# Three quarters of two output tiles moved in between the last attention steps

## Chip, cores and metric

The kernel runs on one core of one Trainium2 chip. The metric is the device time of one execution in microseconds (us); lower is better. TensorE (PE in the profile) multiplies matrices into PSUM, ScalarE (ACT) and VectorE (DVE) work between PSUM and SBUF, GpSimd (POOL) works on SBUF, and SyncE (SP) issues the weight loads.

## The reference, cut to what matters

Three blocks run one after the other on a sequence of 512 tokens with 1024 features. The second block has two layers, each of them a feed-forward part, an attention part and another feed-forward part; the third block has one attention part. The change concerns the three places where attention ends and its output projection begins:

```
# second block, each layer: four differential heads (d) and four pairs of forget-gate heads (f)
x = x + concat([o_f, o_d]) @ w_out        # o_f: features 0 to 511, o_d: features 512 to 1023
x = x + 0.5 * swiglu(rmsnorm(x))          # the next feed-forward part
# third block: gated recurrence (lru) and four pairs of block attention heads (m)
x = x + gate * (concat([y_lru, y_att]) @ w_out)   # y_att: features 512 to 1023
```

## The kernel before, in words

Activations lie transposed: feature tiles of 128 partitions by 512 tokens. Each float32 product is made of three matmuls on rounded parts: high weight by high input, high weight by low input, low weight by high input (`products`, lines 1467 to 1469). So an output tile of 128 features over four input tiles is 12 matmuls of 128x512, and over eight it is 24.

One program is written once as a sequence of calls on an object `on`; it is run five times, once for each engine, and every engine issues its own instructions in that order. No engine overtakes within its queue. Semaphore events tie them together: `wait_ge` names the event that an instruction waits for.

A weight tile goes through three steps: a DMA brings it to one of five raw buffers, ScalarE rounds it into a high part (line 1904), GpSimd subtracts for the low part (line 3181). Both are issued two units ahead of the projection that needs them (`LOOK` is 2), and around these projections there are three slots for rounded weights, so the tile that is three further on takes the slot of the one just used. A call of `T` issues the rounding of the unit two behind it, then the matmuls.

`attend` writes the order of one attention by hand. A job is one pair of heads and one block of 128 query tokens. Its steps are `scores` (line 1817), softmax on VectorE and ScalarE, `weigh`, `turn` (transposes on TensorE, line 1827, then two ScalarE copies out of PSUM, line 2267) and `gather` (weights times values, line 1844). The two buffers that the copies write are shared by all jobs, so the copies of one job wait for the gather of the job before. In the loop a job is turned in the pass before the one that gathers it. `beside` is a generator of other projections that fill TensorE between the steps; near the end it issues the eight tiles `outd` (or `outl`) of the other half of the output projection. The last pair of heads takes its blocks in the order 3, 2, 1, 0.

When a pair of heads is done, `head_out` makes its high part on ScalarE (line 2000) and its low part on VectorE (line 2427). In the third block VectorE first applies a gate (line 3058), and `head_parts` does the rounding. A matmul on input tile c waits for the low part of c.

After `attend` the eight output tiles follow. In the second block `renew` follows each tile: VectorE adds it to the residual (line 2890), ScalarE scales and rounds it, VectorE makes the sums and low parts that the next feed-forward part takes. The call for tile n rounds the weights of tile n+2 on ScalarE, between the `renew` of tile n-1 and that of tile n. In the third block VectorE adds (line 3156) and SyncE stores.

Of the kernel before, what the change touches and what calls it, by code (L numbers as in the profile page):

```python
# [11 lines left out]
S = 512  # L12
# [166 lines left out]
class Dry:  # L179
# [5 lines left out]
    def wait_ge(self, sem, n):  # L185
        return self
# [11 lines left out]
NRAW, LOOK, LEAD = (5, 2, 2)  # L198
# [712 lines left out]
        return ('o', self.tag, *h)  # L911


def attend(on, at, beside):

    scored = weighed = turned = gathered = 0
    total = len(at.jobs)
    pair = lambda j: at.jobs[j][0][0] != 'd'
    while gathered < total:
        if scored < total and pair(scored):  # L920
            if weighed < scored:
                on.weigh(at, *at.jobs[weighed])
                weighed += 1
            on.scores(at, *at.jobs[scored])
            scored += 1
        elif scored < total:
            on.scores(at, *at.jobs[scored])
            scored += 1
        if turned > gathered and (pair(gathered) or turned - gathered > 1 or scored == weighed == turned):
            h, qt = at.jobs[gathered]  # L930
            on.gather(at, h, qt)
            gathered += 1
            if qt == at.blocks(h)[-1]:
                on.head_out(at, h)
                at.out += 1
        if weighed < scored and (scored == total or scored - weighed > 1):
            on.weigh(at, *at.jobs[weighed])
            weighed += 1
        two = turned < total and pair(turned)
        if two:  # L940
            next(beside, None)
        if weighed > turned and (two or weighed - turned > 2 or scored == weighed):
            on.turn(at, *at.jobs[turned])
            turned += 1
        next(beside, None)
    for _ in beside:
        pass


def second(on, k, layer, m):  # L950
    L, scale = (str(layer), m.scale)
# [36 lines left out]
    at = Heads(k, L, [('d', i) for i in range(4)] + [('f', i) for i in range(4)], k.P2, [last, ('lambda', L), ('forgot', L)])  # L988
# [5 lines left out]
    def projections():  # L994

        ready = None

        def enter():
            if ready is not None and ready[0] == 'dqk':
                on.diff_in(L, ready[1], R, last)  # L1000
                on.rope_moves(L, ready[1])
            elif ready is not None:
                on.fox_in(L, ready[1], R, last)
        for name, n in [('dqk', n) for n in (2, 6, 3, 7)] + [('fqk', n) for n in (0, 4, 1, 5, 2, 6, 3, 7)]:
            on.T_part((name, L, n), name + L, n, A, 0, 2)
            enter()
            yield
            on.T_part((name, L, n), name + L, n, A, 1, 2)
            if ready is not None and ready[0] == 'dqk':
                on.rope(L, ready[1])  # L1010
            ready = (name, n)
            yield
        enter()
        yield
        for i in range(4):
            on.diff_parts(at, i)
            if i % 2:
                yield
        for n in range(KT):
            on.T(('outd_' + L, n), 'out' + L, n, at.OA, kt=4, first=4)  # L1020
            on.part(res, n, ('outd_' + L, n))
            yield
            yield
# [10 lines left out]
    def both():  # L1034
        one, two = (projections(), norms())
        while next(one, 'end') != 'end':
            next(two, None)
            yield
    attend(on, at, both())
    m = Ffn('f2_' + L, 'f2i' + L, 'f2o' + L, res.A, res.sum, None, [('filled', ('out2_' + L, 7))], clear=('filled', ('out2_' + L, 0)), before=res)  # L1040
    res.later = (0, 1, 2, 3)
    for n in range(KT):
        on.T(('out2_' + L, n), 'out' + L, n, at.OA, kt=4)
        renew(on, res, n, ('out2_' + L, n), ('filled', ('fqk', L, 7)), m, 0)
    scale = res.sum
    nxt = banked(Sum('fin2' if layer else 'f1_1', k.R[1 - layer], S, ('fox', L, 7), range(8) if layer else (), 2 if layer else 0, [('lo', ('mid', 'f2_' + L), FF - 1)]))
# [19 lines left out]
def third(on, k, res):  # L1066
    last = ('filled', ('d', 'f2_1', 7))
    on.norm3_gain()
    A = k.XA('n3')
    m = Norm(res.twin, k.X, lambda j: ('x', 'f2_1', j), A, lambda j: k.sm[:, j:j + 1], lambda j: k.ada3[:, j:j + 1], [last, ('gain3',)], keep=True, bank=True)  # L1070
    on.roots(res.twin, 4)
    for j in range(1, 11):
        norm(on, m, j)
        if j == 3:
            on.roots(res.sum, 2)
    on.row(res.sum)
    on.lru_loads(last)
    on.lru_rate()
    for n in range(4):
        if n == 0:  # L1080
            on.T2((('xl', 0), 'z3', 0), (('xl', 1), 'z3', 1), A)
        if n > 1:
            on.T(('xl', n), 'z3', n, A)
        on.lru_in(n, last)
        on.lru('taps', n)
        on.final_tile(res, n, 'final2')
    beside = {0: [('gate', 0, 0), ('gate', 0, 1), ('gate', 1, 0), ('gate', 1, 1)], 4: [('gate', 2, 0), ('gate', 2, 1), ('gate', 3, 0), ('gate', 3, 1)], 1: [('decay', 0), ('decay', 1)], 5: [('decay', 2), ('decay', 3)], 6: [('root', 0), ('root', 1), ('root', 2), ('root', 3)]}
    heads = iter([[], [], [(0, 0), (4, 0)], [], [(0, 1), (4, 1)], [(4, 2), (1, 0), (5, 0)], [(1, 1), (5, 1)], [(5, 2), (2, 0), (6, 0)], [(2, 1), (6, 1)], [(6, 2), (3, 0), (7, 0)], [(3, 1), (7, 1)], [(7, 2)]])
    for i, n in enumerate((0, 4, 1, 5, 2, 6, 3, 7)):
        on.T(('z', n), 'z3', 8 + n, A)  # L1090
        on.head_in(n, last)
        for step in beside.get(n, []):
            on.lru(*step)
        if i < 4:
            on.final_tile(res, 4 + i, 'final2')
        for step in next(heads):
            on.head(*step)
    for kp in range(4):
        on.K('v3', 'v3', 0, A, kp, 4)
        for step in next(heads):  # L1100
            on.head(*step)
    for tt in range(4):
        on.value3(tt, last)
    at = Heads(k, 'm', [('m', i) for i in range(4)], k.P3, [last, ('headed', 7), ('head scale', 3), ('lru mult', 3), ('rate',)])
    at.OA, at.old = (k.XA('y3'), [('filled', ('gl', 3))])
    out = Residual('out3', lambda j: k.ada3[:, 16 + j:17 + j], None)

    def projections():

        ready = None  # L1110
        for i in range(8):
            name, w, n = ('gl', 'z3', i - 4) if i > 3 else ('ga', 'ga3', i)
            on.T_part((name, n), w, i, A, 0, 2)
            if ready is not None:
                on.gate_in3(*ready)
            if i > 4:
                on.lru_gate(i - 5)
            yield
            on.T_part((name, n), w, i, A, 1, 2)
            if i % 2:  # L1120
                on.lru('scan', i // 2)
            ready = (name, n)
            yield
        on.gate_in3(*ready)
        on.lru_gate(3)
        for n in range(4):
            on.lru_out(at, n)
            if n % 2:
                yield
        on.head_parts(at, 0)  # L1130
        on.head_parts(at, 1)
        yield
        for n in range(KT):
            on.T(('outl', n), 'out3', n, at.OA, kt=4)
            on.part(out, n, ('outl', n))
            yield
        on.head_parts(at, 2)
    attend(on, at, projections())
    on.head_parts(at, 3)
    for n in range(KT):  # L1140
        on.T(('out3', n), 'out3', n, at.OA, kt=4, first=4)
        on.store(n)


class Engine:


    def __init__(self, k, e, done):
        self.k, self.e, self.done, self.seen = (k, e, done, {})
        self.pos = self.h = 0  # L1150

    def wait_ge(self, *event):

# [41 lines left out]
    def pair(self, m, i):  # L1195

        upper = self.unit('upper', ('T', m.wi, i, 0), 1024)
        lower = self.unit('lower', ('T', m.wi, FF + i, 0), 1024)
        return (m.tag, i)
# [9 lines left out]
    def T_part(self, key, name, n, X, part, of):  # L1209
        if part == 0:  # L1210
            self.weights(*self.unit('split', ('T', name, n, 0), 1024))

    def K(self, key, name, n, X, kp, ntok):
        self.weights(*self.unit('split', ('K', name, n, kp), 1024))
# [204 lines left out]
class Tensor(Engine):  # L1419
# [27 lines left out]
    def T_part(self, key, name, n, X, part, of):  # L1447

        k, w = (self.k, 8 // of)
        if part == 0:  # L1450
            self.open = self.unit('split', ('T', name, n, 0), 1024)
        i, h = self.open
        out = self.bank(*key) if part else self.take(k.banks, *key, hold=True)
        m = self.products(out, i, h, X, range(w * part, w * part + w), 0, S, 0, 7)
        if part == of - 1:
            m.then_inc(*k.filled.inc(('used', h), ('filled', key)))
            k.banks.let(key)

# [1917 lines left out]
```

## Time and profile before

| what | value |
|---|---|
| median of three runs | 3398.5 us |
| the runs | 3394.53, 3398.5, 3404.37 us |
| the profiled execution's own time | 3406.11 us |
| its span | 3404.3 us |
| TensorE matmul, busy share of the span | 97% |
| VectorE, GpSimd, ScalarE | 55%, 48%, 43% |

In a timeline row the first number is the start from the beginning of the span and the second the duration; in brackets is the time for which the engine sat idle just before and the instruction that released it. Matmuls overlap in the pipeline, so the distance between starts, not the duration, is what one costs.

### The profile page before, as it was taken

The numbers are of one execution on the slowest core, as the hardware profiler recorded it, in microseconds if no ns is written. First come the engines' busy times: TensorE is split into PE (matmuls) and PEld (weight loads), VectorE is DVE, ScalarE is ACT, GpSimd is POOL, SyncE is SP. The second block draws the span as 40 slices with busy tenths as digits, with TensorE's granted clock in tenths as the row PEclk, the third lists the DMA queues.
The fourth block names the chain that finished last, engine by engine and source line by source line (L and its number), as shares of the span: only waits on it lengthen the run. The fifth ranks groups of instructions, "written<-read, shape, count | busy, mean of one in ns | idle before, by whom it ended". The sixth has DMA issues, their size and how long they took to land.

```text
span 3404.3 us, 47159 instructions
## 1 busy us (share of the span) xinstructions
PE 3312.1 (97%) x18750; PEld 2801.7 (82%) x18750; DVE 1880.4 (55%) x3348; ACT 1468.2 (43%) x2582; POOL 1644.4 (48%) x952
## 2 busy tenths in 40 slices
PE   8999999999999999999998999999999999999998
PEld 5767788887888889988777999899987769998776
DVE  4366775523222376842667576557624667582555
ACT  4533323523322363533556354444434555352543
POOL 4313445564544455655415565455546246564332
PEclk9999999999999999999999999999999999999999
DMA  7212333442344423334202323332343123333211
GB/s 284 69 49 62 97 96 126 151 148 71 128 153 144 142 87 100 112 100 121 75 32 86 104 100 104 94 113 88 106 112 109 32 60 111 100 103 105 72 62 56
DMA packets 102218, 345.96 MB, mean 102 GB/s; under 512 B 12173, under 2 KB 12557, under 8 KB 101838
## 3 DMA queue, kind: packets, MB, share of 16 engines
q1 hardware_dynamic: 101200, 341.10, 31.1%
q8 instruction: 148, 2.42, 0.3%
q10 hardware_dynamic: 798, 1.85, 0.2%
q14 instruction: 72, 0.59, 0.1%
HBM read 336.08 MB, written 2.10 MB: 99 GB/s over the span
## 4 chain that ended last, share of the span: by engine, by line
PE 87%; DVE 6%; ACT 4%; issue 1%; POOL 1%; DMA 1%; SPq 0%; DVEq 0%; ACTq 0%; POOLq 0%
PE ps L1467 16%; PE ps L1468 16%; PE ps L1469 16%; PE ps L1503 8%; PE ps L1505 8%; PE ps L1504 8%; PE ps L1530 2%; PE ps L1532 2%; PE ps L1531 2%; PE ps L1817 2%; PE ps L1844 1%; POOL t L3181 1%; PE ps L1827 1%; ACT t L1919 1%; DMA t<-in_w_ada 1%
## 5 line engine op out<-in xcount | busy, mean ns | idle before, releaser
L3181 POOL TENSOR_TENSOR t<-t,t 128x1024 fp32r<-128x1024 f32 (+2 forms) x408 | 931.9, 2291 | 1261.4 <-ACT t L1904 1248.8
L1467 PE MATMUL ps<-t,t 128*128 128x512 f32 x2608 | 1045.0, 401 | 13.4 <-POOL t L3181 8.1
L1468 PE MATMUL ps<-t,t 128*128 128x512 f32 x2608 | 1023.3, 392 | 0.0
L1469 PE MATMUL ps<-t,t 128*128 128x512 f32 x2608 | 1021.7, 392 | 0.0
L3191 POOL TENSOR_TENSOR t<-t,t 128x512 fp32r<-128x512 f32 x440 | 570.4, 1325 | 388.4 <-ACT t L1919 388.4
L1503 PE MATMUL ps<-t,t 128*128 128x256 f32 x2464 | 699.0, 284 | 22.2 <-DVE ps L2477 9.4
L1504 PE MATMUL ps<-t,t 128*128 128x256 f32 x2464 | 693.8, 282 | 0.0
L1505 PE MATMUL ps<-t,t 128*128 128x256 f32 x2464 | 693.5, 281 | 0.0
L1467 PEld LDWEIGHTS ps<-t,t 128*128 128x128 f32 x2608 | 492.8, 189 | 141.0 <-issue 24.2
L1469 PEld LDWEIGHTS ps<-t,t 128*128 128x128 f32 x2608 | 492.6, 189 | 108.3
L1468 PEld LDWEIGHTS ps<-t,t 128*128 128x128 f32 x2608 | 493.2, 189 | 99.4 <-issue 1.7
L1904 ACT CAST t<-t 128x1024 fp32r<-128x1024 f32 (+2 forms) x412 | 398.7, 976 | 348.8 <-PE ps L1469 211.2
L1503 PEld LDWEIGHTS ps<-t,t 128*128 128x128 f32 x2464 | 464.6, 189 | 28.3 <-issue 10.7
L1505 PEld LDWEIGHTS ps<-t,t 128*128 128x128 f32 x2464 | 467.7, 190 | 0.0
L1504 PEld LDWEIGHTS ps<-t,t 128*128 128x128 f32 x2464 | 466.3, 189 | 0.2
L1919 ACT CAST t<-t 128x512 fp32r<-128x512 f32 x440 | 255.4, 620 | 207.1 <-DVE t L2450 186.8
L1919 ACT CAST t<-ps 128x512 fp32r<-128x512 f32 x176 | 103.5, 588 | 140.9 <-DVE ps L2440 106.5
L2260 ACT ACTIVATE t<-ps,t 128x128 f32<-128x128 f32 (+3 forms) x160 | 86.6, 544 | 177.9 <-DVE t L3024 66.5
L2721 DVE SCALAR_TENSOR_TENSOR ps<-t,t,ps 128x392 f32<-128x392 f32 (+14 forms) x232 | 159.1, 686 | 6.2
L2450 DVE TENSOR_TENSOR t<-t,ps 128x512 f32<-128x512 f32 x176 | 119.8, 681 | 48.5 <-PE ps L1505 46.4
L1530 PE MATMUL ps<-t,t 128*128 128x512 f32 x336 | 134.7, 401 | 8.0 <-DVE t L2629 4.3
L2457 DVE TENSOR_TENSOR t<-ps,t 128x512 fp32r<-128x512 f32 x176 | 120.7, 686 | 28.8 <-ACT t L1919 25.3
(331 smaller groups left out, 3637.6 us busy)
## 6 DMA issues: line engine op xcount, KB each, us to landing
t<-in_w_f1i SPq DMA_DIRECT2D x88, 512.0 KB, 3.7
t<-in_w_f2i SPq DMA_DIRECT2D x88, 512.0 KB, 3.8
t<-in_w_ada SPq DMA_DIRECT2D x72, 512.0 KB, 4.3
t<-in_w_ffi SPq DMA_DIRECT2D x44, 512.0 KB, 3.7
t<-in_w_f1o SPq DMA_DIRECT2D x32, 512.0 KB, 4.0
t<-in_w_f2o SPq DMA_DIRECT2D x32, 512.0 KB, 4.0
t<-in_w_gate SPq DMA_DIRECT2D x24, 512.0 KB, 4.0
t<-in_w_out SPq DMA_DIRECT2D x48, 256.0 KB, 2.6
```

Of the source, the lines that this page charges most:

```text
L1467: e.matmul(out, wh[:, at], X.hi[c][:, 0:N], start=c == first, stop=False)
L1468: e.matmul(out, wh[:, at], X.lo[c][:, 0:N], start=False, stop=False)
L1469: m = e.matmul(out, wl[:, at], X.hi[c][:, 0:N], start=False, stop=c == final)
L1503: e.matmul(out, wh[:, at], m.A.hi(j, x), start=opens and j == 0, stop=False, skip_group_check=not opens)
L1504: e.matmul(out, wh[:, at], m.A.lo(j, x), start=False, stop=False, skip_group_check=not opens)
L1505: mm = e.matmul(out, wl[:, at], m.A.hi(j, x), start=False, stop=j == 3, skip_group_check=not opens)
L1530: e.matmul(out, X.hi[c][:, at], wh[:, w], start=c == 0, stop=False)
L1904: e.copy(k.WH[k.slot[n]][:, 0:w], k.raw[:, j % NRAW, 0:w]).then_inc(*k.rounded.inc(('rounded', j)))
L1919: e.copy(four(piece_at(k, k.WH, m, i, piece)), src).then_inc(*k.rounded.inc(('rounded', m.tag, i, piece)))
L2721: e.scalar_tensor_tensor((c3 if j == 30 else a3)[:, :, lo:hi], h3[:, :, lo + w - 15:hi + w - 15], param(k, 'conv_w', w * 8 + i), a3[:, :, ...
L3181: e.tensor_tensor(k.WL[k.slot[n]][:, 0:w], k.raw[:, j % NRAW, 0:w], f(k.WH[k.slot[n]][:, 0:w]), ALU.subtract).then_inc(*k.rest.inc(('rest' ...
L3191: e.tensor_tensor(four(piece_at(k, k.WL, m, i, piece)), src, four(f(piece_at(k, k.WH, m, i, piece))), ALU.subtract).then_inc(*k.rest.inc(( ...
```

## The change

Of output tiles 0 and 1 the products over the first three of the four input tiles (the first three pairs of heads) are issued inside the last passes of the loop in `attend`, through a second generator `fill`. One step of it is one input tile for one output tile: three matmuls. There are six steps in each attention. One step is taken after each gather once all scores are issued, and two after each turn. After `attend`, tiles 0 and 1 only get their products over the last pair of heads. Their two PSUM banks are held from the first step on. All three attentions are changed; the number of instructions is not.

```diff
-def attend(on, at, beside):
+def attend(on, at, beside, fill):
...
             if qt == at.blocks(h)[-1]:
                 on.head_out(at, h)
                 at.out += 1
+            if scored == total and gathered < total:
+                next(fill, None)
...
             on.turn(at, *at.jobs[turned])
             turned += 1
+            if scored == total:
+                next(fill, None)
+                next(fill, None)
         next(beside, None)
     for _ in beside:
         pass
+    for _ in fill:
+        pass
+
+
+def begun(on, at, name, w, first):
+
+    for c in range(first, first + 3):
+        for n in range(2):
+            on.T_some((name, n), w, n, at.OA, (c,), first=first)
+            yield
...
-    attend(on, at, both())
+    attend(on, at, both(), begun(on, at, 'out2_' + L, 'out' + L, 0))
...
     for n in range(KT):
-        on.T(('out2_' + L, n), 'out' + L, n, at.OA, kt=4)
+        if n < 2:
+            on.T_some(('out2_' + L, n), 'out' + L, n, at.OA, (3,))
+        else:
+            on.T(('out2_' + L, n), 'out' + L, n, at.OA, kt=4)
         renew(on, res, n, ('out2_' + L, n), ('filled', ('fqk', L, 7)), m, 0)
...
-    attend(on, at, projections())
+    attend(on, at, projections(), begun(on, at, 'out3', 'out3', 4))
     on.head_parts(at, 3)
     for n in range(KT):
-        on.T(('out3', n), 'out3', n, at.OA, kt=4, first=4)
+        if n < 2:
+            on.T_some(('out3', n), 'out3', n, at.OA, (7,), first=4)
+        else:
+            on.T(('out3', n), 'out3', n, at.OA, kt=4, first=4)
         on.store(n)
...
@@ class Engine
+    def T_some(self, key, name, n, X, ks, first=0, kt=4):
+
+        if ks[0] == first:
+            self.opened[key] = self.unit('split', ('T', name, n, first), 128 * kt)
+            i, h = self.opened[key]
+            self.weights(i, h - LOOK)
+        if ks[-1] == first + kt - 1:
+            self.weights(*self.opened[key])
...
@@ class Tensor(Engine)
+    def T_some(self, key, name, n, X, ks, first=0, kt=4):
+
+        k, final = (self.k, first + kt - 1)
+        if ks[0] == first:
+            self.opened[key] = self.unit('split', ('T', name, n, first), 128 * kt)
+        i, h = self.opened[key]
+        out = self.take(k.banks, *key, hold=True) if ks[0] == first else self.bank(*key)
+        m = self.products(out, i, h, X, ks, first, S, first, final)
+        if ks[-1] == final:
+            m.then_inc(*k.filled.inc(('used', h), ('filled', key)))
+            k.banks.let(key)
```

## Rows read from the trace of the kernel before

**Rows 1.** The page: busy time, share of the span, instructions.

```profile
PE 3312.1 (97%) x18750; PEld 2801.7 (82%) x18750; DVE 1880.4 (55%) x3348; ACT 1468.2 (43%) x2582; POOL 1644.4 (48%) x952
```

**Rows 2.** Busy time by stretch: end of attention, layers 0 and 1; then eight output tiles.

```profile
1791.92:1801.09 9.17, 6.95 (x79) 5.22 (x77) 2.66 (x12) 5.29 (x15) 1.28 (x1) 1.00 0.08 29
2761.24:2770.41 9.17, 6.95 (x79) 5.22 (x77) 2.65 (x12) 5.29 (x15) 1.28 (x1) 1.00 0.12 29
1801.09:1823.78 22.69, 22.69 (x99) 17.66 (x97) 15.57 (x33) 16.56 (x33) 15.89 (x12) 1.00 0.39 127
```

**Rows 3.** Timeline of TensorE, layer 0: the last turns and gathers, output tiles 0 and 3.

```profile
1791.92 1.09 PE L1827 MATMUL ps<-t,t 128*128 128x128 f32 x8
1793.26 1.09 PE L1844 MATMUL ps<-t,t 128*64 128x128 f32 x16 [0.24 <-ACT t L2267]
1794.29 0.88 PE L1827 MATMUL ps<-t,t 128*128 128x128 f32 x6
1795.61 1.09 PE L1844 MATMUL ps<-t,t 128*64 128x128 f32 x16 [0.45 <-ACT t L2267]
...
1800.72 0.44 PE L1844 MATMUL ps<-t,t 128*64 128x128 f32 x4 [0.61 <-ACT t L2267]
1801.09 0.50 PE L1467 MATMUL ps<-t,t 128*128 128x512 f32 x1
...
1809.45 0.40 PE L1467 MATMUL ps<-t,t 128*128 128x512 f32 x1
```

**Rows 4.** Timeline of ScalarE in the same stretch.

```profile
1794.39 1.07 ACT L2267 COPY t<-ps 128x512 f32<-128x512 f32 x2 [0.57 <-PE ps L1844]
1795.35 0.60 ACT L2000 CAST t<-ps 128x512 fp32r<-128x512 f32 x1
...
1801.19 0.59 ACT L2000 CAST t<-ps 128x512 fp32r<-128x512 f32 x1 [0.62 <-PE ps L1844]
...
1807.23 0.62 ACT L1904 CAST t<-t 128x512 fp32r<-128x512 f32 x1
```

**Rows 5.** Timeline of VectorE in the same stretch.

```profile
1795.99 0.69 DVE L2427 TENSOR_TENSOR t<-ps,t 128x512 fp32r<-128x512 f32 x1 [1.58 <-ACT t L2000]
1801.82 0.69 DVE L2427 TENSOR_TENSOR t<-ps,t 128x512 fp32r<-128x512 f32 x1 [5.14 <-ACT t L2000]
1804.15 0.69 DVE L2890 SCALAR_TENSOR_TENSOR t<-ps,t 128x512 f32<-128x512 f32 x1 [1.65 <-PE ps L1469]
```

**Rows 6.** Timeline of GpSimd in the same stretch: low parts of weights.

```profile
1791.95 1.28 POOL L3181 TENSOR_TENSOR t<-t,t 128x512 fp32r<-128x512 f32 x1 [2.97 <-ACT t L1904]
...
1807.93 1.30 POOL L3181 TENSOR_TENSOR t<-t,t 128x512 fp32r<-128x512 f32 x1 [4.26 <-ACT t L1904]
```

**Rows 7.** Timeline of TensorE, third block: the last gathers, output tiles 0 and 1.

```profile
3372.31 0.88 PE L1844 MATMUL ps<-t,t 128*64 128x128 f32 x12 [1.70 <-ACT t L2267]
...
3374.62 1.12 PE L1844 MATMUL ps<-t,t 128*64 128x128 f32 x8 [0.84 <-ACT t L2267]
...
3376.82 0.70 PE L1844 MATMUL ps<-t,t 128*64 128x128 f32 x4 [0.46 <-ACT t L2267]
3377.44 0.79 PE L1467 MATMUL ps<-t,t 128*128 128x512 f32 x1
...
3381.87 0.40 PE L1467 MATMUL ps<-t,t 128*128 128x512 f32 x1
```

**Rows 8.** Timeline of VectorE, third block: low part of the last heads.

```profile
3378.92 0.69 DVE L2427 TENSOR_TENSOR t<-t,t 128x512 fp32r<-128x512 f32 x1 [0.68 <-ACT t L2000]
```

**Rows 9.** Busy time by stretch; the column after POOL's is the granted clock.

```profile
1832.00:1834.00 2.00, 0.81 (x6) 0.60 (x6) 2.00 (x4) 2.00 (x5) 2.00 (x2) 1.00 0.00 0
1834.00:1836.00 2.00, 1.04 (x5) 1.04 (x6) 2.00 (x2) 0.69 (x2) 2.00 (x2) 0.65 0.00 0
3374.00:3376.00 2.00, 1.38 (x10) 1.04 (x10) 0.52 (x3) 0.48 (x2) 0.00 (x0) 0.51 0.00 0
3380.00:3382.00 2.00, 2.00 (x8) 1.59 (x8) 0.00 (x0) 0.00 (x0) 0.76 (x1) 0.79 0.00 0
```

More of the change, by code:

```diff
@@ L1150, in __init__ @@
         self.pos = self.h = 0
+        self.opened = {}
     def wait_ge(self, *event):
```

## Prediction

> **What bounds the kernel now.** First the page: TensorE is busy for 97% of the span and no other engine for more than 55% [rows 1]. So time can only be won where TensorE idles or runs at the lower of its two clock levels, and it is lost wherever a new wait stands in its queue. Then the busy time of the stretches that the change touches: from the transposes behind the last scores to the first output tile TensorE is busy 6.95 of 9.17 us, in both layers alike, so 2.2 us are idle; in the eight output tiles behind it TensorE idles for nothing [rows 2]. Then TensorE's timeline of the end of attention [rows 3]: turns and gathers alternate, and each gather waits 0.24 to 0.61 us for ScalarE's copies. ScalarE's own copies wait for the gather before [rows 4], since two buffers are shared: gather, copies, gather is one chain, and the transposes stand beside it. In the third block the waits before gathers are longer, 1.70, 0.84 and 0.46 us [rows 7].
>
> About 0.3%, 10.2 us, is what a measurement of this kernel can tell from no change.
>
> **The change, part by part.** No instruction is added or removed. The weight loads, their rounding and the low parts on GpSimd stay at their places in each queue: the weights of output tiles 0 and 1 are ready before the fills (GpSimd ends the second at 1793.23 [rows 6]; with one fill and eight transposes ahead of it that weight is wanted at about 1793.7), so SP, ScalarE and GpSimd get nothing new to wait for there. The two PSUM banks come from finished jobs. I cost these edits at nothing; if the weight came late, its first user would wait under 1 us.
>
> *One fill.* From 1801.09 to 1809.45 lie 36 matmuls of the kind [rows 3]: 0.232 us each, three cost 0.70, the six fills of an attention 4.18.
>
> *First gap in a layer.* Three fills, 2.09 us, stand before the gather that began at 1793.26; 0.24 of idle takes part of it. The gather starts 1.85 later.
>
> *Second gap.* Before the next gather come one fill, a turn and two fills on the third input tile. That tile is what the gather at 1793.26 finishes. Its low part was there at 1795.99 + 0.69 = 1796.68 [rows 5], behind the two copies and the rounding on ScalarE [rows 4]: 3.42 after the gather's start. TensorE gets there after gather (1.03), fill (0.70) and turn (0.88), 2.61. It stalls 0.81, then does two fills, and the gather comes 3.42 + 1.39 = 4.81 after the one before instead of 2.35: 2.46 later. Queued behind that stall are the gather, and through the shared buffers the next copies, so everything behind moves too. The fills are used up here; the three later gaps stay as they are. Attention ends 1.85 + 2.46 = 4.31 later, for 4.18 of work moved.
>
> *The cover that goes.* Before, the last heads' output was rounded while TensorE did three quarters of tile 0: the low part came at 1801.82 + 0.69 = 1802.51 [rows 5], 1.42 after TensorE began the tile, and nothing was seen of it. Now the only products left in tiles 0 and 1 need just this part: TensorE stalls 1.42. After 1.39 more for both tiles, tile 2 takes 2.78.
>
> *The weights of tile 3.* Their rounding stands on ScalarE behind the renewal of tile 0 (at 1807.23, [rows 4]); GpSimd ends at 1809.23 [rows 6] and TensorE begins tile 3 at 1809.45 [rows 3]: 0.22 to spare. The renewal starts with VectorE's addition, 3.06 after the start of the output tiles now [rows 5], 0.51 after the start of the tile's twelfth matmul; in the new order it is 1.42 + 0.46 + 0.51 = 2.39, so 0.67 sooner, but from a start 4.31 later: 3.64 late. The weights come at 1812.87, TensorE is free at 1805.40 + 1.42 + 1.39 + 2.78 = 1810.99. It stalls 1.9, and tile 3 begins 3.4 late. From there weights and tiles run in step as before.
>
> The sum for one layer: new stalls 0.81 + 1.42 + 1.9 = 4.1, less the idle that is filled, 0.24 + 0.45 = 0.7: 3.4 on TensorE; by the renewal's start 3.6. I take 3.5. The bounds: 0, if ScalarE, idle for 22.69 - 16.56 = 6.1 us of the output tiles [rows 2], lets the renewals catch up; and 3.6 with no catching up. I take a value near the upper, because each rounding stands behind a renewal and comes with 0.22 to spare. Behind the tiles, in the first products of the feed-forward part, VectorE is busy throughout while TensorE is 0.81 of 2.00 us [rows 9]: a delay handed to VectorE is not made good there.
>
> *Third block.* The idle filled is 0.84 + 0.46 = 1.30. The first three input tiles are long finished, so there is no stall between the fills. The cover is worse: the last heads' low part is ready at 3378.92 + 0.69 = 3379.61 [rows 8], 2.17 after output tile 0 began [rows 7]. No renewal follows, and the rounding for tile 2 (about 1.9 us behind the last high part, by the lengths in [rows 4, 6]) comes just as tiles 0 and 1 end. So 0.9 is lost at an unchanged clock. The clock is half in this stretch: the granted clock is 0.51 in 3374 to 3376 and 0.79 in 3380 to 3382 [rows 9], which puts the half level, 1.2 GHz, from about 3374.0 to 3380.8. Tile 0 took 4.43 there instead of 2.78 [rows 7], 1.65 lost. With TensorE filled from 3372.31 on the full level may return sooner: all of it would make -0.8, none +0.9. I take 0, the middle.
>
> A rule weighed: the TensorE clock. [Rows 9] show TensorE busy 0.81 of 2.00 us, and in the next two the granted clock at 0.65; [rows 2] show 2.2 us of idle, in pieces up to 0.61, over 9.17 us at 1.00. The new stalls, 0.61 and 1.42 with one short gather between and then 1.9, lie between the two. The Trainium skill (TensorE: Matmul & The Clock Gate, A second HAM failure mode) tells of a kernel whose short idles between groups of matmuls let the clock swing between the two levels. By that rule each layer would come out as in rival A; the trace agrees with it in [rows 9] and not in [rows 2].
>
> The sum: 2 x 3.5 + 0 = +7.0. The profiled execution would go from 3406.1 to 3413.1. It lies 7.6 above the median of the runs shown; the difference is carried over, 3398.5 + 7.0 = 3405.5.
>
> **The rivals.**
>
> A: the clock falls at the new stalls; slower. The place is output tiles 0 to 5 of each layer. A half-clock stretch as long as that in the third block, 6.8 us, costs up to 3.4; one that takes only a tile's worth, 1.65. For it speaks the 1.70 of idle before the clock at 0.51 [rows 7, 9], against it [rows 2]. It decides from one tile's worth in each layer on: 7.0 + 3.3 = 10.3. At the full price it is 7.0 + 6.8 = 13.8: 3412.
>
> B: the delay is made good. ScalarE's 6.1 us of idle lets the renewals catch up, TensorE's stall at tile 3 shrinks, and the change does almost nothing: +1, 3399.5. Against it: the 0.22 to spare.
>
> C: the fills do what they seem to do. All idle before gathers is filled and no stall takes its place: at most 2.2 + 2.2 + 1.3 = 5.7, with the clock of tile 0 7.4, short of 10.2. A middle of -3 gives 3395.5. It needs the last low part not to be waited for, and the rows say that it is.
>
> **How the numbers follow.** The forecast (+4 to +10, no clock stretch that counts) 0.45, A 0.37, B 0.12, C 0.06. The time is the forecast's, 3405.5. The range goes from 3397, which leaves out most of C, to 3416, A with a third stretch. Slower by over 0.3% is A, 0.37; faster is the edge of C, 0.02; within 0.3% is the rest, 0.61.
>
> **What would show it.** Right: in the new trace no idle before the gather that began at 1793.26; a wait of TensorE for line 2427 of about 0.8 between fills, and of about 1.4 (2.2 in the third block) before the last quarter of tile 0; a wait for line 3181 of near 1.9 at tile 3; attention's end 4.3 later. Wrong: tile 3 without a wait (then B), the granted clock under 1.00 in output tiles 0 to 5 (then A), or no wait for line 2427 (then C). A half-clock stretch elsewhere that comes or goes between executions would shift the time by a like amount without the change having caused it.

## The result and the profile after

The changed kernel took 3406.7 us (median of 11 runs, 3404.99 to 3413.29), the kernel before 3398.5 (11 runs, 3394.29 to 3404.37). The ratio is 1.0024 [1.0016, 1.0032]: 8.2 us slower, 5.4 to 10.9 by the interval. The forecast was 3405.5, 7.0 slower than before and so within 0.3% of it. The prediction took 10.2 us as the least that a measurement of this kernel can tell from no change; with eleven runs of each kernel 8.2 can be told as well.

The profiled execution took 3405.18 us with a span of 3403.4, 0.9 under that of before, although the median rose. As the prediction says, the profiled execution of before lay 7.6 above its median; that of after lies 1.5 below. So whole spans say nothing here, and what follows compares **stages**: from the start of the last scores of an attention to the first product of the next feed-forward part, and in the third block to the end of VectorE's last addition. The last scores of layer 0 and that first product, TensorE's timeline, before:

```profile
1790.58 0.61 PE L1817 MATMUL ps<-t,t 80*128 80x128 f32 x4
...
1823.78 0.35 PE L1503 MATMUL ps<-t,t 128*128 128x256 f32 x1
```

The same view after (scores are now line 1860, turns 1870, gathers 1887, the projection's products 1510 to 1512, the feed-forward's 1546), with what lies between:

```profile
1784.27 0.61 PE L1860 MATMUL ps<-t,t 80*128 80x128 f32 x4
...
1786.42 1.04 PE L1870 MATMUL ps<-t,t 128*128 128x128 f32 x8
1787.21 0.48 PE L1510 MATMUL ps<-t,t 128*128 128x512 f32 x1
1787.53 0.40 PE L1511 MATMUL ps<-t,t 128*128 128x512 f32 x1
...
1788.77 1.09 PE L1887 MATMUL ps<-t,t 128*64 128x128 f32 x16
1789.80 0.51 PE L1510 MATMUL ps<-t,t 128*128 128x512 f32 x1
...
1790.62 0.82 PE L1870 MATMUL ps<-t,t 128*128 128x128 f32 x6
1792.26 0.50 PE L1510 MATMUL ps<-t,t 128*128 128x512 f32 x1 [0.82 <-DVE t L2470]
...
1793.85 1.09 PE L1887 MATMUL ps<-t,t 128*64 128x128 f32 x16
...
1798.97 0.44 PE L1887 MATMUL ps<-t,t 128*64 128x128 f32 x4 [0.61 <-ACT t L2310]
1800.81 0.55 PE L1510 MATMUL ps<-t,t 128*128 128x512 f32 x1 [1.40 <-DVE t L2470]
1801.15 0.63 PE L1511 MATMUL ps<-t,t 128*128 128x512 f32 x1
1801.58 0.63 PE L1512 MATMUL ps<-t,t 128*128 128x512 f32 x1
...
1804.56 0.40 PE L1510 MATMUL ps<-t,t 128*128 128x512 f32 x1
...
1807.36 0.50 PE L1510 MATMUL ps<-t,t 128*128 128x512 f32 x1 [0.56 <-POOL t L3224]
...
1821.80 0.36 PE L1546 MATMUL ps<-t,t 128*128 128x256 f32 x1
...
2773.11 0.50 PE L1510 MATMUL ps<-t,t 128*128 128x512 f32 x1 [1.40 <-DVE t L2470]
...
2779.25 0.50 PE L1510 MATMUL ps<-t,t 128*128 128x512 f32 x1 [0.16 <-POOL t L3224]
```

The gather at 1788.77 no longer waits, where that of before waited 0.24 [rows 3]. Two waits for the low part (line 2470, formerly 2427) are new: 0.82 in the middle of the fills, 1.40 before tile 0's last quarter. Tile 3 waits 0.56 for its weights, in layer 1 (the last two rows) 0.16. From 1801.15 to 1804.56 matmuls start 0.43 apart instead of 0.23. The stage is 37.53 long, against 33.20. VectorE's timeline after, the low parts and the addition that starts the renewals:

```profile
1791.51 0.69 DVE L2470 TENSOR_TENSOR t<-ps,t 128x512 fp32r<-128x512 f32 x1 [2.99 <-ACT t L2043]
1800.06 0.69 DVE L2470 TENSOR_TENSOR t<-ps,t 128x512 fp32r<-128x512 f32 x1 [7.86 <-ACT t L2043]
1802.24 0.69 DVE L2933 SCALAR_TENSOR_TENSOR t<-ps,t 128x512 f32<-128x512 f32 x1 [1.49 <-PE ps L1512]
```

The first addition stands 17.97 behind the last scores; before, 1804.15 [rows 5] less 1790.58, 13.57. The stretch of slow matmuls is a matter of the clock: busy time by stretch after, two rows of layer 0 and two of layer 1; the granted clock is the number behind POOL's column.

```profile
1801.00:1803.00 2.00, 2.00 (x6) 1.56 (x6) 0.69 (x1) 0.03 (x1) 0.91 (x1) 0.53 0.07 15
1803.00:1805.00 2.00, 2.00 (x7) 1.56 (x6) 0.80 (x3) 1.61 (x3) 0.00 (x0) 0.61 0.38 122
2774.00:2776.00 2.00, 2.00 (x6) 1.55 (x5) 0.69 (x1) 1.15 (x3) 0.21 (x1) 0.50 0.31 92
2776.00:2778.00 2.00, 2.00 (x7) 1.58 (x6) 1.80 (x5) 1.56 (x4) 0.10 (x1) 0.66 0.10 39
```

In these tiles the kernel before had 1.00 [rows 2]. So TensorE fell to the half level, 1.2 GHz, just behind the 1.40 wait in both layers, and stayed there for 3.4 us. The third block after, TensorE's timeline:

```profile
3372.95 0.88 PE L1887 MATMUL ps<-t,t 128*64 128x128 f32 x12 [1.70 <-ACT t L2310]
...
3379.56 0.44 PE L1887 MATMUL ps<-t,t 128*64 128x128 f32 x4
...
3382.17 0.50 PE L1510 MATMUL ps<-t,t 128*128 128x512 f32 x1 [2.16 <-DVE t L2470]
```

Here the last two gathers no longer wait, as they did for 0.84 and 0.46 [rows 7], a wait of 2.16 stands before tile 0's last quarter, and the clock is full where it was half [rows 9]. The stretch that contains them, after:

```profile
3372.00:3382.00 10.00, 7.05 (x48) 5.07 (x48) 3.77 (x15) 4.01 (x13) 0.02 (x1) 1.00 0.01 2
```

The page and the view of waits show the sums over the whole kernel. The page's first line, after:

```profile
PE 3307.5 (97%) x18750; PEld 2798.6 (82%) x18750; DVE 1885.1 (55%) x3348; ACT 1469.2 (43%) x2582; POOL 1641.0 (48%) x952
```

The waits of TensorE after, for which line it waited: us in total, times, longest.

```profile
PE ps L1510 <- POOL t L3224: 8.4, 7, 2.4
PE ps L1510 <- DVE t L2470: 8.3, 7, 2.2
PE ps L1887 <- ACT t L2310: 7.7, 9, 2.7
```

No share on the page has moved [rows 1]; the new waits are seen only by line. Of the seven for the low part (line 2470), two stand some 40 us ahead of these stages (1744.51 and 2716.78, 0.8 each), where the kernel before waits too (0.38 and 0.83). New are the other five: twice 0.82, twice 1.40 and 2.16, 6.6 in all.

All kernels of the study by stage (us from the start of the last scores; the first two columns for layer 0 and layer 1), with the ratio of their runs to runs of before taken beside them (medians of those 3398.5, 3398.94 or 3400.45):

| kernel | first addition | stage of a layer | third block | ratio |
|---|---|---|---|---|
| before | 13.57, 13.57 | 33.20, 33.19 | 31.75 | 1 |
| after | 17.97, 17.57 | 37.53, 37.11 | 30.18 | 1.0024 [1.0016, 1.0032] |
| layers_only | 17.98, 17.60 | 37.53, 37.16 | 29.51 | 1.003 [1.002, 1.0039] |
| third_only | 13.58, 13.57 | 33.22, 33.20 | 30.20 | 1.0005 [0.9996, 1.0013] |
| two_inputs | 15.08, 15.05 | 34.62, 34.60 | 31.84 | 1.0014 [1.0006, 1.0023] |
| pad | 17.55, 17.56 | 37.09, 37.11 | 32.04 | 1.0025 [1.0015, 1.0035] |
| pad_weights_first | 17.56, 17.55 | 38.26, 37.09 | 31.78 | 1.0031 [1.0018, 1.0043] |
| tile_one_only | 16.32, 16.31 | 35.85, 35.86 | 31.96 | 1.0016 [1.0007, 1.0025] |
| third_spread | 13.60, 13.58 | 33.21, 33.20 | 26.81 | 0.9987 [0.9979, 0.9996] |
| late_one | 13.20, 13.22 | 32.84, 32.83 | 26.79 | 0.9986 [0.9977, 0.9994] |

Of after's stages, layer 0 is 4.33 longer, layer 1 3.92, the third block 1.57 shorter: +6.7, inside the interval of the runs. Every stage is read from one execution of its kernel.

### The profile page after: what moved, and what is told of

Its sections match the earlier page's. It is cut to its first block, busy times and chain, and to the rows that moved or that the text cites. A ratio compares the mean times of both kernels' runs of the same rounds, so it can differ in the third digit from the quotient of the medians.

```text
span 3403.4 us, 47157 instructions
## 1 busy us (share of the span) xinstructions
PE 3307.5 (97%) x18750; PEld 2798.6 (82%) x18750; DVE 1885.1 (55%) x3348; ACT 1469.2 (43%) x2582; POOL 1641.0 (48%) x952
## 4 chain that ended last, share of the span: by engine, by line
PE 88%; DVE 6%; ACT 3%; DMA 1%; issue 1%; POOL 1%; SPq 0%; DVEq 0%; ACTq 0%; POOLq 0%
PE ps L1510 17%; PE ps L1512 16%; PE ps L1511 16%; PE ps L1546 8%; PE ps L1548 8%; PE ps L1547 8%; PE ps L1573 2%; PE ps L1574 2%; PE ps L1575 2%; PE ps L1860 2%; PE ps L1887 1%; PE ps L1870 1%; ACT t L1962 1%; POOL t L3224 1%; DMA t<-in_w_ada 1%
## 5 line engine op out<-in xcount | busy, mean ns | idle before, releaser
L1546 PEld LDWEIGHTS ps<-t,t 128*128 128x128 f32 x2464 | 464.7, 189 | 28.5 <-issue 9.6
```

Of the source, the lines that this page charges most:

```text
L1546: e.matmul(out, wh[:, at], m.A.hi(j, x), start=opens and j == 0, stop=False, skip_group_check=not opens)
```

## The experiments

**One part alone.** layers_only leaves the third block as before, third_only the layers.

```diff
# layers_only
-    attend(on, at, projections(), begun(on, at, 'out3', 'out3', 4))
+    attend(on, at, projections(), iter(()))
...
# third_only
-    attend(on, at, both(), begun(on, at, 'out2_' + L, 'out' + L, 0))
+    attend(on, at, both(), iter(()))
# in both, the tiles behind that attention are whole again: on.T(..., kt=4)
```

> The change in the two layers of the second block alone; the third block's attention as before. The stage is read from the start of the last scores to the first product of the feed-forward part: 33.2 us before. Theory (new waits of 0.8 and 1.4 on low parts, then renewals that start late): 37.0 to 37.6 in each layer, so +8 in all, 3406.5. Rival (the loss in the layers is made good later in the feed-forward part): the stage is as long, but the whole is within 3 of before. Rival (the third block has a part in the loss): +5 or less here.

> The change in the third block alone. From the start of the last scores to the end of the last residual addition it was 31.75 us before and 30.18 with the whole change, where the clock was full. Theory: idle of 1.30 filled, 2.17 waited for the last low part, the rest is the clock: between 30.2 (full clock) and 32.6 (half clock as long as before); time within 2 of before. Rival (the fills help here by more than the idle they fill): under 29.5 and -3 or better.

Measured: 3408.76 us and 3401.1, beside 3398.94 for before. The layers hold the whole loss, and it is not made good later: the run is 6.8 to 13.3 slower by the interval, the two stages 8.3. The third block alone, 1.4 faster to 4.4 slower, can't be told from no change. Its stage is 30.20, with a wait of 2.17, at the full clock. Whether that is a gain depends on the clock of the block it replaces: the unchanged third block took 29.51 at the full level (layers_only) and 31.75 to 32.04 with a stretch at the half level (before, two_inputs, pad, pad_weights_first, tile_one_only). So the change costs 0.7 at an equal clock and wins 1.6 against an execution whose clock fell. Busy time of the same ten microseconds, before and in layers_only, both with that block unchanged:

```profile
3372.00:3382.00 10.00, 8.39 (x43) 6.12 (x44) 3.33 (x13) 3.27 (x11) 1.27 (x1) 0.66 0.01 2
3372.00:3382.00 10.00, 6.89 (x50) 4.92 (x49) 4.91 (x20) 5.24 (x17) 1.29 (x1) 1.00 0.01 2
```

**Less moved, a cover kept.** Only the first two input tiles are moved, and the third, done behind the last gather, covers the last low part.

```diff
# two_inputs (the third block as before)
-    for c in range(first, first + 3):
+    for c in range(first, first + 2):
...
+    for n in range(2):
+        on.T_some(('out2_' + L, n), 'out' + L, n, at.OA, (2,))
```

> In the layers only two of the four input tiles are begun in the attention (four fills instead of six); the third input tile's products of output tiles 0 and 1 are done right behind the last gather, ahead of those that need the last heads. Third block as before. Theory (the waits on low parts are what costs): no wait of TensorE for a low part in the fills or at output tile 0; attention ends about 2.1 later than before instead of 4.5, the first residual addition comes 0.4 sooner behind it; stage 34.9 in each layer, +3.4 in all. Rival (moving products between gathers costs by itself, each fill its whole length): 36 or more. Rival (the held banks cost): as with six fills, 37 to 37.6.

Measured: 3404.03 us. No wait for the low part is left in these stages, and still each is 1.4 longer. The attention ends 2.09 later (12.67 behind the last scores, before 10.58), tile 0 is done 0.58 sooner behind it, and the first addition comes 1.51 later. VectorE's timeline of it:

```profile
1802.25 0.69 DVE L2932 SCALAR_TENSOR_TENSOR t<-ps,t 128x512 f32<-128x512 f32 x1 [1.06 <-PE ps L1511]
```

So the stalls aren't the whole cost: 1.4 of the 4 us comes with four fills and no stall, from work moved ahead of the attention's end; the rest went together with the two stalls and the other two fills. Both rivals, 36 or more and 37 or more, fall.

**The clock kept full.** Six products that nobody reads run in the 1.40 wait of each layer, so that TensorE is busy there; no other part of the layers is changed. The third block is as before.

```diff
# pad, behind attend
+    on.pad(at, ('out2_' + L, 1))
...
# class Tensor; on the other engines pad does nothing
+    def pad(self, at, key):
+        k, e = (self.k, self.e)
+        i, h = self.opened[key]
+        b = self.take(k.banks, 'pad', at.tag)
+        for j in range(6):
+            m = e.matmul(b, k.WH[k.slot[h]][:, 0:128], at.OA.hi[0][:, 0:S], start=j == 0, stop=j == 5)
+        m.then_inc(*k.filled.inc(('filled', ('pad', at.tag)), ('free', ('pad', at.tag))))
```

> As the change in the layers alone, with six matmuls more behind the last gather, into a bank that nothing reads, so that TensorE is busy while it waits for the last low part. Theory (the end of the stage follows the start of the renewals): the granted clock stays at 1.00 in output tiles 0 to 2, the wait for the weights of tile 3 grows from 0.2 to 0.6 to over 1.2, and the stage is 0 to 0.6 shorter than without the six, 36.8 to 37.5. Rival (the half-clock stretch is what costs): the stage is 1.5 or more shorter. Rival (the clock falls all the same): 37 to 37.6 with half clock again.

Measured: 3407.06 us, not to be told from after. Its busy time by stretch, over the end of the extra products and the last quarters of tiles 0 and 1 in layer 0:

```profile
1803.00:1805.00 2.00, 2.00 (x10) 1.49 (x9) 0.69 (x1) 0.82 (x2) 1.10 (x1) 1.00 0.00 0
```

VectorE's timeline of it, the first addition:

```profile
1805.08 0.69 DVE L2940 SCALAR_TENSOR_TENSOR t<-ps,t 128x512 f32<-128x512 f32 x1 [1.06 <-PE ps L1519]
```

Its timeline of TensorE, tile 3 and the stage's end:

```profile
1810.18 0.51 PE L1517 MATMUL ps<-t,t 128*128 128x512 f32 x1 [1.70 <-POOL t L3231]
...
1824.62 0.35 PE L1553 MATMUL ps<-t,t 128*128 128x256 f32 x1
```

The clock is 1.00 from the last scores to the stage's end, in both layers, and tile 3 now waits 1.70. After's 0.56 and 0.16 are what the half level left of it: eight spacings of 0.43 instead of 0.23 take 1.57 more, and 1.70 - 1.57 + 0.40 = 0.53 in layer 0, 1.70 - 1.57 = 0.13 in layer 1. The 0.40 is the one price of the fall: in layer 0 it came before tile 0's last products, so that the first addition stood at 17.97 instead of 17.55; in layer 1, one matmul group later (2773.91), it cost nothing.

**The wait at tile 3 moved.** As pad, with the last quarters of tiles 0 and 1 both issued before the first renewal, so that the rounding for tile 3 stands ahead of it on ScalarE.

```diff
# pad_weights_first, beside pad's edit
+    for n in range(2):
+        on.T_some(('out2_' + L, n), 'out' + L, n, at.OA, (3,))
     for n in range(KT):
-        if n < 2:
-            on.T_some(('out2_' + L, n), 'out' + L, n, at.OA, (3,))
-        else:
+        if n > 1:
             on.T(('out2_' + L, n), 'out' + L, n, at.OA, kt=4)
```

> The layers as in pad (the changed order with six extra products that nobody reads in the 1.40 wait, so that the clock stays full; no part of the result depends on them), third block as before. The last quarters of output tiles 0 and 1 are both issued before the renewal of tile 0, so that the rounding of tile 3's weights stands ahead of that renewal on ScalarE instead of behind it. Theory (the chain of renewals on VectorE and ScalarE sets the end of the stage, and the wait at tile 3 is only where TensorE feels it): the wait of 1.70 at tile 3 goes, one of about 1 appears at tile 4 or 5, and the stage from the last scores to the feed-forward's first products is 36.5 to 37.1, against pad's 37.1. Rival (the wait at tile 3 is itself the cost): the stage is 35.4, the run 3.4 under pad.

Measured: 3410.35 us, beside 3400.45 for before. The wait at tile 3 is gone and stands at tile 4, in both layers; its timeline:

```profile
1812.69 0.47 PE L1517 MATMUL ps<-t,t 128*128 128x512 f32 x1 [1.84 <-POOL t L3231]
...
1814.54 0.63 PE L1518 MATMUL ps<-t,t 128*128 128x512 f32 x1
...
1817.53 0.43 PE L1519 MATMUL ps<-t,t 128*128 128x512 f32 x1
...
2784.85 0.47 PE L1517 MATMUL ps<-t,t 128*128 128x512 f32 x1 [1.84 <-POOL t L3231]
2785.16 0.40 PE L1518 MATMUL ps<-t,t 128*128 128x512 f32 x1
```

Layer 1's stage is 37.09 with the wait here or there: the wait is where TensorE feels the chain of renewals, not a cost of its own. The rival, 35.4, falls. Layer 1 of after says the same: its wait is 0.16 where pad's is 1.70, slower matmuls took the rest, and both stages are 37.11. In layer 0 the clock went to the half level from 1814.2 to 1817.5, with no later wait to hide it, and the stage is 1.17 longer than in pad; in layer 1 the same wait was followed by no fall. Why one and not the other stays open.

**Tile 1 alone moved.** Tile 0 stays whole behind the attention and covers the low part as before.

```diff
# tile_one_only (at.plan names the steps, counted from the last job, behind which a fill is taken;
# T_open rounds tile 0's weights ahead of tile 1's; its text and a condition for it in T_some are not shown)
+    at.plan = {('gather', -6): 1, ('turn', -4): 1, ('turn', -2): 1}
+    def second_tile():
+        on.T_open(('out2_' + L, 0), 'out' + L, 0)
+        for c in range(3):
+            on.T_some(('out2_' + L, 1), 'out' + L, 1, at.OA, (c,))
+            yield
+    attend(on, at, both(), second_tile())
...
-            on.T_some(('out2_' + L, n), 'out' + L, n, at.OA, (3,))
+            on.T_some(('out2_' + L, n), 'out' + L, n, at.OA, (3,) if n else (0, 1, 2, 3))
```

> The layers only, third block as before. The three fills of output tile 1 alone are done during the attention, tile 0 is done whole behind it, so that tile 0 covers the late low part as before the change; half of the work is moved. Theory (what counts is when the renewal of tile 0 starts, 3.06 after the end of the attention, and the attention ends later by what is moved into it): no wait of TensorE at tile 0, attention's end 1.7 to 2.2 later, the stage 34.7 to 35.4 against 33.2 before; the run 3 to 4.5 us slower than before. Rival (TensorE's total counts, and a fill that takes idle is won): the stage 32.5 to 33.3, the run as before or up to 1.4 faster.

Measured: 3406.69 us, 2.4 to 8.5 slower than before. The delay of a stage was larger than expected (35.85, not 34.7 to 35.4), since the first fill came before its weights were there; TensorE's timeline, with tile 3 below:

```profile
1789.36 0.47 PE L1522 MATMUL ps<-t,t 128*128 128x512 f32 x1 [1.36 <-POOL t L3236]
...
1807.99 0.50 PE L1522 MATMUL ps<-t,t 128*128 128x512 f32 x1 [1.70 <-POOL t L3236]
```

What was to be told apart is told all the same. There is no wait at tile 0, the attention ends 2.72 later (13.30, before 10.58), the first addition 2.75, and the stage is 2.65 and 2.67 longer. That three fills are gone from the tiles behind bought nothing. The rival, 32.5 to 33.3, falls.

**Where a fill does help.** third_spread (layers as before) puts four fills of the third block into its gaps of 0.92, 1.70 and 0.84 and holds three back as cover. late_one adds one fill in each layer, in the last gap, 0.61, and leaves three quarters of tile 0 as cover.

```diff
# both kernels, third block
+    at.plan = {('gather', -4): 1, ('scores', -1): 2, ('turn', -2): 1}
+    def begun3():
+        for c in (4, 5):
+            for n in range(2):
+                on.T_some(('out3', n), 'out3', n, at.OA, (c,), first=4)
+                yield
+    attend(on, at, projections(), begun3())
+    for n in range(2):
+        on.T_some(('out3', n), 'out3', n, at.OA, (6,), first=4)
+    on.T_some(('out3', 2), 'out3', 2, at.OA, (4,), first=4)
...
+        elif n == 2:
+            on.T_some(('out3', n), 'out3', n, at.OA, (5, 6, 7), first=4)
# late_one, layers (here begun yields the one fill, tile 0 over input tile 0)
+    at.plan = {('gather', -2): 1}
...
-        if n < 2:
-            on.T_some(('out2_' + L, n), 'out' + L, n, at.OA, (3,))
+        if n < 1:
+            on.T_some(('out2_' + L, n), 'out' + L, n, at.OA, (1, 2, 3))
```

> Third block only; the layers as before. Four of the six fills are put one by one into the gaps before gathers that the profile of before shows (one into 0.92, two into 1.70, one into 0.84), and the third input tile of output tiles 0 and 1 and the first of tile 2 are held back behind the last gather, about 2.1 us of products that need nothing late. Theory (idle filled counts, as long as something covers the late low part): from the last scores to the end of the last addition of VectorE 27 to 28.5 us, against 29.5 of the block as before at the full clock and 30.2 of the changed one; no wait of TensorE for the low part at tile 0, or under 0.3; the run 1.5 to 4 us under before, 3395 to 3397.5. Rival (the chain of VectorE's weighing and ScalarE's copies sets the end, TensorE's idle doesn't count): 29.3 to 30.2 in that stage, the time as before within 1.

> The third block as in third_spread, and in each layer one single fill (output tile 0, first input tile) in the last of the gaps, the 0.61 before the last gather; the other three quarters of tile 0 come after it and cover the late low part. Theory (a fill in a gap delays the attention only by what it exceeds the gap, 0.1 to 0.2, and the renewal of tile 0 starts 0.7 of products sooner behind it): the stage of a layer 32.6 to 33.0 against 33.2, a wait of at most 0.7 before tile 0's last quarter, the run within 1 of third_spread, and 2 to 5 under before. Rival (any fill costs the chain its whole 0.8): the stage 33.6 to 33.9, the run 1 to 1.5 over third_spread.

Measured: 3395.07 and 3395.39 us, beside 3400.45 for before. TensorE's timeline of third_spread: the first of the two fills in the 1.70 gap, the last gather, tile 0 behind it.

```profile
3367.21 0.50 PE L1521 MATMUL ps<-t,t 128*128 128x512 f32 x1 [0.31 <-ACT t L2314]
...
3372.51 0.44 PE L1898 MATMUL ps<-t,t 128*64 128x128 f32 x4 [0.56 <-ACT t L2321]
3372.88 0.50 PE L1521 MATMUL ps<-t,t 128*128 128x512 f32 x1
```

No wait for the low part is left, and the stage is 26.81, 2.7 less than the unchanged block at the full clock (a little under the expected 27 to 28.5). The runs gain 1.4 to 7.1 by the interval, 5.4 at the median, where 1.5 to 4 was expected. That fits what the profiles show, half-level stretches in five unchanged blocks of six and none in this one's two; the clock by stage of the other runs is not on record, so this reason is not shown. The timeline of TensorE of late_one, layer 0, the fill, the last gather and the stage's end:

```profile
1795.96 0.50 PE L1523 MATMUL ps<-t,t 128*128 128x512 f32 x1
...
1796.85 0.44 PE L1900 MATMUL ps<-t,t 128*64 128x128 f32 x4
...
1819.34 0.35 PE L1559 MATMUL ps<-t,t 128*128 128x256 f32 x1
```

VectorE's timeline of it, the first addition:

```profile
1799.70 0.69 DVE L2946 SCALAR_TENSOR_TENSOR t<-ps,t 128x512 f32<-128x512 f32 x1 [1.06 <-PE ps L1525]
```

The fill takes the 0.61 gap whole; the attention ends 0.21 later, the first addition comes 0.37 and 0.35 sooner, and the stages are 0.36 shorter. The rival, 33.6 to 33.9, falls. The runs of the two kernels can't tell 0.7 us apart; the stages can.

## Why the prediction was right, and where it wasn't

*What sets the end.* The prediction gave two readings of a layer, TensorE's stalls (3.4) and the renewal's start (3.6). The table decides for the second: from the first addition to the stage's end it is 19.53 to 19.64 in 19 of the 20 layers of the ten kernels, 19.63 before; the other is layer 0 of pad_weights_first, with its half-level stretch. The first addition came 4.40 and 4.00 later, the stages are 4.33 and 3.92 longer; in late_one it came 0.37 sooner, and the stage is 0.36 shorter. The link between them is the rounding of tile 3's weights, 3.08 behind the addition before (1804.15 to 1807.23 [rows 4, 5]) and after (1802.24 to 1805.32). ScalarE's timeline after:

```profile
1805.32 0.62 ACT L1947 CAST t<-t 128x512 fp32r<-128x512 f32 x1
```

The step was right, "no catching up" included, and rival B falls with it. Rival C falls with the waits: 0.24 and 0.45 of idle are filled, but 0.82, 1.40 and 0.56 stand in their place.

*The size of that step.* 3.64 was predicted; with tile 0 at the full clock it is 3.98 and 3.99 (pad) and 4.00 (layer 1 of after). Two terms were too small. A fill was priced 0.70 from back-to-back products; in the timeline after, 1789.80 to 1790.62 is 0.82 for one and 1787.21 to 1788.77 is 1.56 for two, since the step from one kind of matmul to another takes 0.1 more: 1787.21 to 1787.53 is 0.32, where 0.23 is usual. So six cost 4.8, not 4.18. By the prediction's own working that makes 4.8 + 0.82 - 0.69 = 4.9; measured, the attention ends 4.57 later instead of 4.31, because the turn of 1786.42 now hands over after 0.79 where it had taken 1.10 before idle [rows 3]. And the first addition gained 0.57 on the attention's end, not 0.67.

*The single waits* came as worked out: 0.82 (0.81) between the fills, 1.40 (1.42) before the last quarter, 2.16 (2.17) in the third block, none at the gather that used to wait 0.24, and the later gaps of 0.46, 0.46 and 0.61 as before.

*The wait at tile 3* was predicted at 1.9 and was 0.56 and 0.16. The term was right at the full clock, 1.70 in pad, two_inputs and tile_one_only. What the prediction didn't see is that a fall of the clock would use up this very wait. The sum on TensorE counted it as 1.9 of its 4.1 of stalls; it is the renewal's delay, seen from another engine. By the sign "tile 3 without a wait (then B)" the 0.16 of layer 1 would nearly have spoken for B, though that stage is 3.92 longer.

*Rival A.* Its mechanism occurred and its price did not. The granted clock fell, to 0.50 and 0.53 over 2 us, in tiles 0 to 2 of both layers, and the prediction's test, "the granted clock under 1.00 in output tiles 0 to 5 (then A)", would have called A right. pad shows the price: 0.44 of the stage in layer 0 and none in layer 1, not 1.65 to 3.4 each. The test named a clock and no path. The Trainium skill (TensorE: Matmul & The Clock Gate, A second HAM failure mode) tells of a kernel whose short idles between groups of matmuls let the clock swing between its two levels; after's rows agree, with 3.4 us at the half level behind a 1.40 wait. What a swing costs the stages show: 1.17 in layer 0 of pad_weights_first, where no wait follows that could take it up, and 0.44 or nothing in after, where the wait at tile 3 does.

*The third block.* The middle of -0.8 and +0.9 was taken, 0. At an equal clock it is +0.67 to +0.69 (30.18 and 30.20 against 29.51), near the end named for that case; against the profiled execution it is -1.57, beyond the other end, because the half level cost the block 2.24 (31.75 against 29.51) and not the 1.65 read from tile 0 alone. Changed third blocks had the full clock in four profiles of four, unchanged ones in one of six; what decides it is not shown. The runs of third_only, 1.4 faster to 4.4 slower, don't show the gain of 1.57.

*The sum.* +7.0 was predicted, +6.7 stands in the stages, of which the layers are 8.25 (7.0 predicted) and the third block -1.57 (0). So the layers were 1.25 too low and the third block 1.57 too high, and that the sum fits is luck; the interval of the runs, 5.4 to 10.9, holds both values.

## What to carry to other kernels

Before work is moved into the idle gaps of the busiest engine, find the instruction on which the stage's end hangs at a fixed distance; here it was VectorE's first addition, and every us that the fills pushed it back came out at the end, though TensorE was busy for 97% of the span. Here a fill was won where it was about the size of its gap and where enough was left behind the last step to cover the last input's latency: one in 0.61 won 0.36, four in 3.46 won 2.7, six in 0.69 of idle lost 4. A wait that a change adds may be only the place where a delay shows; move it, as here from tile 3 to tile 4, and see whether the end moves, before it is counted.

## What the runs showed of the hardware

- One wait of TensorE of 1.40 us, with gaps of 0.46 to 0.61 shortly before it, was followed by 3.4 us at the half level (granted 0.50) in after and layers_only, in both layers. Waits of 1.70 at tile 3 (pad, two_inputs, tile_one_only) were followed by none; one of 1.84 was in layer 0 of pad_weights_first and was not in layer 1.
- In each of three such stretches (after from 1801.15 and from 2773.91, pad_weights_first from 1814.15) matmuls of 128x512 started 0.43 apart instead of 0.23.
- The same instructions in the same order, the unchanged third block, had the half level for a while in five profiles (31.75 to 32.04) and the full one throughout in a sixth (29.51), 2.2 to 2.5 us apart.
